# The sample attention's cache steps: three unrolled laps of 16 groups written as one register loop

## The chip, the cores and the metric

The kernel runs on one core of one Trainium2 chip. The metric is the device time of one execution in microseconds (us), the median of three runs. The core's engines each have their own instruction stream: TensorE (PE, with its weight loads shown as PEld), VectorE (DVE), ScalarE (ACT), GpSimd (POOL) and SyncE (SP), which here issues most of the DMAs. In rows of the profile a name with a "q" behind it (DVEq, SPq) is the sequencer of that engine, the part that reads the instruction stream, evaluates waits, does register arithmetic and branches.

## The reference

One inference step of a decoder layer. New tokens of a prompt (1024 and 16 meta tokens) and of 8 running sequences (8 tokens each) go through one projection. It feeds a pooling mixer and a latent attention of 8 heads. Then come an output projection and an MLP. The part that the change touches is the attention of the running sequences over their paged cache:

```python
def one_seq(args):                        # 8 sequences, 4096 cached positions each
    pt, qi, ci, kri = args
    c_all = concat([cache_kv_latent[pt].reshape(past, KV_LORA), ci])
    kr_all = concat([cache_k_rope[pt].reshape(past, QK_ROPE), kri])
    k = mla_keys(c_all, kr_all, w_uk, ...)      # project 256 -> 8 heads x 64, append rope, RMS norm
    s = einsum('qhd,khd->hqk', qi, k) * SCALE
    p = softmax(where(mask, s, -inf))
    ctx = einsum('hqk,kr->qhr', p, c_all)
    return einsum('qhr,rhv->qhv', ctx, w_uv)
```

## The kernel before

The program has four stages one after the other: the front (projections), the prompt attention, the sample attention and the tail (output projection and MLP). All five engines run each stage, and order among them is kept by counting semaphores alone: `eng.wait_ge(S[name], n)` holds an engine until the semaphore has reached n, and semaphores only ever grow, so n depends on the step.

**The sample attention.** The cache of a sequence is 32 pages of 128 positions. Four pages make a group, 8 groups make a sequence, and 64 groups (`NG`) make the stage. The groups go through a ring of 16 buffers (`RING`, two sequences). Step g is a software pipeline. In it PE turns group g's latents (eight transposes, L1294) and rope keys (L1304), and computes key norms and scores of group g-1 page by page. A page is 12 matmuls in three-pass form (helper `three_pass`, L104 to L106), six of 320 columns and six of 256. PE also does one rope product, and the context product of group g-12 (L1251, L1255) between page 1 and page 2. ACT copies the turned latents (`cTh`, L1358) and squares each page's keys (`sq`, L1340). DVE makes the low halves (`cTl`, L1416), adds rope to the scores (`summed`, L1404), reduces the squares (L1406) and closes a step with `krss` (L1491) and `var` (L1494). POOL scales scores and splits the context operand. Page j+2 on PE may start only when DVE has emptied the banks of page j (`S["summed"]`). SP loads a group's pages, four page numbers read from the page table (L1155), each followed by two DMAs (L1156, L1157), as soon as the context product has freed the buffer (`S["ctx"]`).

**How the steps are written out.** `steps` calls an engine's step function once for each g. The first 16 steps are the fill, in which `valid(x)` leaves out work of groups before the first. The last five drain the pipeline. The 48 between are all alike but for the wait counts, the page numbers and the sequence number, which are constants in the unrolled text. They are 16 steps (a lap) repeated three times.

**The tail** is written the other way already: its `steps` emits 6 steps as they are, and then a register loop `with eng.Fori(1, NS // LAP) as lap` (L1771) whose body is 6 steps, run seven times by PE, ACT and DVE. SP has a loop of its own there (L1743). Wait counts in such a body are worked out from the loop's register by the engine's sequencer (ALU_OP and FUSED_REGOPS in the rows), and the body ends with an addition and a COMPARE_BRANCH to its first instruction.

Of the kernel before, what the change touches and what calls it, by code (L numbers as in the profile page):

```python
# [48 lines left out]
NG = NSEQ * NPAGE // GP  # L49
GS = NPAGE // GP  # L50
RING = 2 * GS
# [1098 lines left out]
def load_pages(nc, A, C, c_tile, kr_tile, arrived, g):  # L1150


    cache, krope = A["cache_kv_latent"], A["cache_k_rope"]
    for j in range(GP):
        page = nc.sync.value_load(C["pages"][0:1, bass.ds(g * GP + j, 1)], min_val=0, max_val=cache.shape[0] - 1)  # L1155
        nc.sync.dma_start(c_tile[:, j, :], cache[bass.ds(page, 1), :, :].rearrange("a p n -> p (a n)")).then_inc(arrived, 16)  # L1156
        nc.sync.dma_start(kr_tile[:, j, :], krope[bass.ds(page, 1), :, :].rearrange("a p n -> p (a n)")).then_inc(arrived, 16)  # L1157


def sample_attention(nc, A, C, ps, B, arrived):  # L1160
# [7 lines left out]
    with ExitStack() as ctx:  # L1168
# [11 lines left out]
        S = {k: sem("sa_" + k) for k in (  # L1180
            "transposed", "hi", "lo", "krt", "krhi", "krlo", "q", "kn", "sq", "ssq", "rope", "ropec", "summed", "krsq", "krss",
            "var", "sd", "rinv", "scaled", "most", "newcopied", "pair", "lmax", "turned", "top", "spread", "gmax",
            "shifted", "exp", "prob_hi", "prob_lo", "const", "c_hi", "c_lo", "c_lo_end", "ctx", "ctx_copied", "folded", "rden", "ctxn",
            "mask0", "mask1", "mask", "zeros", "ones", "uk_hi", "uk_lo", "ukt", "ukt_c", "qr_hi", "qr_lo", "qt", "qt_hi", "qt_lo",
            "new", "s_new", "sums", "end")}
# [7 lines left out]
        @block.sync  # L1193
        def _(sp):
            def load(k, g):
                load_pages(nc, A, C, c_ring[k], kr_ring[:, k % GS], group_in[k], g)

            for k in range(EARLY, RING):
                if k >= GS:
                    sp.wait_ge(S["krt"], k - GS + 1)  # L1200
                    sp.wait_ge(S["krsq"], k - GS + 1)
                load(k, k)
            for g in range(RING, NG):
                sp.wait_ge(S["ctx"], g - RING + 1)
                load(g % RING, g)

        def steps(emit):

            def program(eng):
                for g in range(RING):  # L1210
                    emit(eng, g, g, 0, lambda x, g=g: 0 <= g - x, True)
                for g in range(RING, NG):
                    emit(eng, g % RING, g, g // RING, lambda x: True, True)
                for g in range(NG, NG + 5):
                    emit(eng, g % RING, g, g // RING, lambda x, g=g: g - x < NG, False)
            return program
# [927 lines left out]
```

## Time and profile before

| | |
|---|---|
| median of 3 runs | 2212.88 us (2212.47 to 2216.06) |
| the profiled execution | 2212.47 us, of which the span 2210.7 us |
| PE busy / DVE / ACT / POOL | 2093.6 / 1181.0 / 813.9 / 377.6 us |
| granted PE clock, mean over the span | 0.977 |
| sample attention, fill (16 steps) | 703.7 to 836.9 us |
| its three laps of 16 steps | 836.9 to 984.4, 1131.8 and 1279.3 us |
| its drain | to about 1321 us |
| tail | to the end |

The span is from the first to the last instruction, and the 1.8 us around it are outside the program's instructions. A lap's share of time is found by the starts of the first transposes (L1294) of steps 16, 32, 48 and of the first step after the last lap. Busy time of an engine is not its bound: what counts is which engine's idle time lies on the path to the end.

### The profile page before, as it was taken

To read this page: it belongs to the slowest core of one execution; us is meant where nothing else is said; L and a number is where in the kernel's file an instruction comes from. 1 tells how busy PE (TensorE), PEld (TensorE's weight loads), DVE (VectorE), ACT (ScalarE), POOL (GpSimd) and SP (SyncE) were. 2 spreads that over 40 slices of the span, in tenths; PEclk is the share of its full clock that TensorE was granted. 3 is DMA by queue.
4 is the path that set the end of the run, shared out by engine and by line. 5 is a ranking of instruction groups with operands and counts; after the bars stand their busy time and mean duration, and the time that the engine had idled before them with its cause. 6 is when DMAs were issued, how large, how long until landed. Compare 5 with 4: busy or idle time off the path is not lost. (4 is left out here: it accounts for less than half of the span.)

```text
span 2210.7 us, 35185 instructions
## 1 busy us (share of the span) xinstructions
PE 2093.6 (95%) x12673; PEld 1922.5 (87%) x12673; DVE 1181.0 (53%) x2358; ACT 813.9 (37%) x1585; POOL 377.6 (17%) x436
## 2 busy tenths in 40 slices
PE   6998999969988999999999979999999999999998
PEld 5887999958877999999999958898989998989997
DVE  3764311146765777677767744444454445454444
ACT  4552111145553556566656633322121112221111
POOL 1110000024441145355535501000000000000000
PEclk8999999989998999999999989999999999999999
DMA  4233222134422312222222107021111111111102
GB/s 151 85 85 83 59 79 80 64 102 130 122 73 61 89 32 63 71 63 65 64 71 63 39 32 259 1 77 39 58 38 57 38 38 38 57 38 57 38 19 86
DMA packets 146191, 152.69 MB, mean 69 GB/s; under 512 B 50695, under 2 KB 122103, under 8 KB 145022
## 3 DMA queue, kind: packets, MB, share of 16 engines
q1 hardware_dynamic: 140325, 128.28, 19.8%
q0 software_dynamic: 5728, 22.65, 3.3%
q8 instruction: 77, 1.26, 0.2%
q14 instruction: 61, 0.49, 0.1%
HBM read 124.77 MB, written 25.97 MB: 68 GB/s over the span
## 5 line engine op out<-in xcount | busy, mean ns | idle before, releaser
L104 PE MATMUL ps<-mh,f_w1h 128*128 128x384 f32 (+1 forms) x768 | 250.6, 326 | 0.0
L106 PE MATMUL ps<-mh,f_w1l 128*128 128x384 f32 (+1 forms) x768 | 250.5, 326 | 0.0
L105 PE MATMUL ps<-ml,f_w1h 128*128 128x384 f32 (+1 forms) x768 | 250.3, 326 | 0.0
L1340 ACT ACTIVATE sq<-ps 128x512 f32<-128x512 f32 x256 | 153.1, 598 | 231.1 <-PE ps L106 231.1
L1892 ACT ACTIVATE tail_room<-ps 128x384 f32<-128x384 f32 (+1 forms) x96 | 45.5, 474 | 502.1 <-PE ps L106 502.1
L1937 DVE TENSOR_TENSOR t_m<-t_m,ps 128x512 f32<-128x512 f32 x256 | 171.5, 685 | 107.0 <-PE ps L106 107.0
L105 PE MATMUL ps<-f_late_l,f_late_h 128*128 128x512 f32 x512 | 199.9, 390 | 0.0
L106 PE MATMUL ps<-f_late_h,f_late_l 128*128 128x512 f32 x512 | 199.8, 390 | 0.0
L104 PE MATMUL ps<-f_late_h 128*128 128x512 f32 x512 | 199.3, 389 | 0.0
L1917 DVE TENSOR_TENSOR tail_room<-tail_room 128x384 f32<-128x384 f32 (+1 forms) x96 | 51.5, 536 | 253.8 <-ACT tail_room L1892 253.8
L104 PE MATMUL ps<-wq,cTh 128*128 128x320 f32 x512 | 171.9, 336 | 2.1 <-DVE g_attn_b L1404 2.1
L1406 DVE TENSOR_REDUCE ss<-sq 128x8 f32<-128x512 f32 x256 | 172.8, 675 | 0.0
L105 PE MATMUL ps<-wq,cTh 128*128 128x320 f32 x512 | 159.3, 311 | 0.0
L106 PE MATMUL ps<-wq,cTl 128*128 128x320 f32 x512 | 158.7, 310 | 0.0
L104 PEld LDWEIGHTS ps<-mh,f_w1h 128*128 128x128 f32 x768 | 144.2, 188 | 1.9
L105 PEld LDWEIGHTS ps<-ml,f_w1h 128*128 128x128 f32 x768 | 144.2, 188 | 1.8
L106 PE MATMUL ps<-w_late,cTl 128*128 128x256 f32 x512 | 145.1, 283 | 0.0
L105 PE MATMUL ps<-w_late,cTh 128*128 128x256 f32 x512 | 144.8, 283 | 0.0
L1404 DVE TENSOR_TENSOR g_attn_b<-ps,g_attn_b 128x64 f32<-128x64 f32 x256 | 56.8, 222 | 164.1 <-ACT sq L1340 162.9
L106 PEld LDWEIGHTS ps<-mh,f_w1l 128*128 128x128 f32 x768 | 144.1, 188 | 0.0
L104 PE MATMUL ps<-w_late,cTh 128*128 128x256 f32 x512 | 143.5, 280 | 0.0
L106 PEld LDWEIGHTS ps<-f_late_h,f_late_l 128*128 128x128 f32 x512 | 96.1, 188 | 20.2
(348 smaller groups left out, 5051.7 us busy)
## 6 DMA issues: line engine op xcount, KB each, us to landing
f_raw<-in_w_ff SPq DMA_DIRECT2D x32, 1024.0 KB, 5.3
c_ring<-in_cache_kv_latent SPq DMA_DIRECT2D x192, 128.0 KB, 2.0
m_raw<-in_w_in SPq DMA_DIRECT2D x20, 512.0 KB, 4.0
gated<-gate POOLq DMA_DIRECT2D x8, 1088.0 KB, 5.2
pa_gm<-gated SPq DMA_DIRECT2D x16, 512.0 KB, 4.9
c_early<-in_cache_kv_latent SPq DMA_DIRECT2D x64, 128.0 KB, 2.0
fr_x<-in_x_prompt SPq DMA_DIRECT2D x8, 512.0 KB, 3.5
mixed<-pa_mixed SPq DMA_DIRECT2D x16, 256.0 KB, 2.1
```

What stands on the lines that cost most here:

```text
L104: nc.tensor.matmul(out, lh, rh, start=first, stop=False)
L105: nc.tensor.matmul(out, lh, rl, start=False, stop=False)
L106: return nc.tensor.matmul(out, ll, rh, start=False, stop=last)
L1340: nc.scalar.activation(sq[:, j % 2, :].rearrange("p (a n) -> p a n", a=2), ps[:, kn_bank(j):kn_bank(j) + 2, 0:HALF], ACT.Square).then_inc( ...
L1404: nc.vector.tensor_tensor(summed[:, p1, j * HQ:(j + 1) * HQ], ps[:, kn_bank(j), HALF:HALF + HQ], rope[:, p1, j * HQ:(j + 1) * HQ], ALU.add ...
L1406: nc.vector.tensor_reduce(ss[:, p1, j * H:(j + 1) * H], sq[:, j % 2, :].rearrange("p (h d) -> p h d", d=NOPE), AX.X, ALU.add).then_inc(S[" ...
L1892: nc.scalar.activation(z[:, a, 0:w], ps[:, 2 * par + a, 0:w], ACT.Relu).then_inc(S["relu"], 1)
L1917: nc.vector.tensor_tensor(z[:, a, 0:w], z[:, a, 0:w], z[:, a, 0:w], ALU.mult).then_inc(S["z"], 1)
L1937: nc.vector.tensor_tensor(part, part, ps[:, bank, :], ALU.add).then_inc(S["y"], 1)
```

## The change

The three laps become one loop body with a register counter, on SP, PE, ACT, DVE and POOL alike. Each engine has its own loop and its own register `lap`, 1 to 3. The body is the same 16 steps. The fill and the drain stay unrolled. No instruction that computes or moves data is added or taken away, and semaphores, buffers and the order of the work stay.

```diff
-            for g in range(RING, NG):
-                sp.wait_ge(S["ctx"], g - RING + 1)
-                load(g % RING, g)
+            with sp.Fori(1, NG // RING) as lap:
+                for k in range(RING):
+                    sp.wait_ge(S["ctx"], lap * RING + (k - RING + 1))
+                    load(k, lap * RING + k)
 
         def steps(emit):
 
             def program(eng):
                 for g in range(RING):
                     emit(eng, g, g, 0, lambda x, g=g: 0 <= g - x, True)
-                for g in range(RING, NG):
-                    emit(eng, g % RING, g, g // RING, lambda x: True, True)
+                with eng.Fori(1, NG // RING) as lap:
+                    for k in range(RING):
+                        emit(eng, k, lap * RING + k, lap, lambda x: True, True)
                 for g in range(NG, NG + 5):
                     emit(eng, g % RING, g, g // RING, lambda x, g=g: g - x < NG, False)
             return program
```

## Rows read from the trace of the kernel before

**Rows 1.** The page: engines over the span, PE and its clock in 40 slices.
```profile
PE 2093.6 (95%) x12673; PEld 1922.5 (87%) x12673; DVE 1181.0 (53%) x2358; ACT 813.9 (37%) x1585; POOL 377.6 (17%) x436
...
PE   6998999969988999999999979999999999999998
...
PEclk8999999989998999999999989999999999999999
```
**Rows 2.** Windows: the second ring lap, then one lap of the tail's loop.
```profile
core 0: us, PE busy (x) PEld busy (x) DVE busy (x) ACT busy (x) POOL busy (x), PEclk, DMA share, GB/s
...
984.40:1131.80 147.40, 144.34 (x1105) 140.83 (x1105) 104.53 (x265) 90.66 (x174) 69.14 (x74) 1.00 0.25 66
...
1687.50:1782.30 94.80, 94.80 (x497) 86.03 (x496) 45.45 (x69) 18.56 (x28) 0.00 (x0) 1.00 0.14 44
```
**Rows 3.** Waits in the first ring lap: PE, PEld and SP.
```profile
PE ps L1251 <- DVE prob_hl L1410: 3.1, 2, 1.5
...
PEld ps L1255 <- issue: 0.8, 2, 0.4
PEld ps L1304 <- issue: 0.8, 2, 0.4
...
SPq L1155 <- PE ps L1251: 39.4, 16, 4.7
```
**Rows 4.** Lines L1771 (tail loop) and L1936 (a wait in it): control instructions, ns.
```profile
L1771 DVEq FUSED_REGOPS  x7: 51/51/51, 1498.3 to 2067.7; - x7
...
L1771 ACTq COMPARE_BRANCH  x7: 40/45/45, 1587.0 to 2156.1; - x7
...
L1771 PEldq COMPARE_BRANCH  x7: 83/215/233, 1589.4 to 2158.5; - x7
...
L1771 DVEq COMPARE_BRANCH  x7: 50/56/72, 1593.1 to 2162.2; - x7
...
L1936 DVEq ALU_OP  x210: 40/40/40, 1508.4 to 2161.2; - x105
```
**Rows 5.** Timeline of DVE: an unrolled tail step, then the same one looped.
```profile
1491.86 1.24 DVE L1928 TENSOR_TENSOR f_late_l<-tail_room,f_late_h 128x384 fp32r<-128x384 f32 x2
1493.01 1.30 DVE L1937 TENSOR_TENSOR t_m<-t_m,ps 128x512 f32<-128x512 f32 x2
...
1586.80 1.23 DVE L1928 TENSOR_TENSOR f_late_l<-tail_room,f_late_h 128x384 fp32r<-128x384 f32 x2
1587.94 1.28 DVE L1937 TENSOR_TENSOR t_m<-t_m,ps 128x512 f32<-128x512 f32 x2
```
**Rows 6.** DMA queues: packets, MB, share; the second ring lap, then the whole span.
```profile
q8 instruction: 9, 0.15, 0.4%
q14 instruction: 11, 0.09, 0.2%
...
q8 instruction: 77, 1.26, 0.2%
```
**Rows 7.** DMA in 1600 to 2150 us, all queues; and landing of the ring's rope loads.
```profile
q1 hardware_dynamic: 14621, 23.78, 13.4%
issues: line engine op xcount, KB each, median us to landing
f_raw<-in_w_ff SPq DMA_DIRECT2D x22, 1024.0 KB, 5.3
...
DMA to landing us min/median/max: 1.6/1.8/4.3
```
**Rows 8.** Timeline of PE around its first branch, at 1589.4 us.
```profile
1589.41 0.39 PE L106 MATMUL ps<-f_late_h,f_late_l 128*128 128x512 f32 x1
...
1592.61 0.39 PE L1865 MATMUL ps<-f_late_h 128*128 128x512 f32 x1
```
**Rows 9.** Timelines across the end of the second ring lap: PE, then DVE.
```profile
1131.82 0.28 PE L106 MATMUL ps<-w_late,cTl 128*128 128x256 f32 x1
1131.94 1.04 PE L1294 MATMUL ps<-ident,c_early 128*128 128x128 f32 x8
...
1137.08 0.31 PE L104 MATMUL ps<-wq,cTh 128*128 128x320 f32 x1
...
1133.82 0.19 DVE L1494 TENSOR_TENSOR var<-ss,krss 128x32 f32<-128x32 f32 x1
1133.92 1.28 DVE L1416 TENSOR_TENSOR cTl<-ps,cTh 128x512 fp32r<-128x512 f32 x2
...
1135.32 0.21 DVE L1404 TENSOR_TENSOR g_attn_b<-ps,g_attn_b 128x64 f32<-128x64 f32 x1
```
**Rows 10.** Timeline of PE: two stalls; and the windows right behind and around them.
```profile
1285.80 0.52 PE L104 MATMUL ps<-wq,cTh 128*128 128x320 f32 x1 [2.07 <-DVE g_attn_b L1404]
...
880.13 0.39 PE L1251 MATMUL ps<-ch,prob_hl 128*128 128x258 f32 x1 [1.52 <-DVE prob_hl L1410]
...
1286.00:1289.40 3.40, 3.40 (x15) 3.40 (x15) 1.26 (x4) 0.43 (x1) 0.63 (x1) 0.50 0.00 0
...
876.00:882.00 6.00, 4.48 (x32) 3.76 (x31) 5.96 (x13) 4.42 (x8) 5.91 (x12) 1.00 0.12 28
```

## The prediction

> **What bounds the kernel now.** I read the page first. PE works 95% of the span at nearly the full clock, and nothing else comes near it [rows 1]. Next the windows of one ring lap: 16 steps take 147.4 us, PE is busy 144.3 of them, DVE 104.5, ACT 90.7, POOL 69.1 [rows 2]. Then the waits of a lap. PE stands 3.1 us for DVE's split of the probabilities, twice, and its weight loads wait 0.8 us at two places each for instructions to be issued [rows 3]. So this stage is a train of matmuls with small holes. Anything that delays another engine is free until a hole opens in that train, and what touches PE's own stream is paid at once.
>
> **What the change removes.** Program text, and with it nothing that PE waits for. PE's instructions come by DMA on the queue named instruction: 77 packets for the program, 1.26 MB, 16 KB each, and 9 of them in a ring lap [rows 6]. A lap has 1105 matmuls and as many weight loads, 2210 instructions, so a packet carries about 250. All this is fetched ahead: the issue waits of a lap are four of 0.4 us [rows 3], too few for nine packets, and the array does not stand for them, since its idle 147.4 - 144.3 = 3.1 us [rows 2] all have DVE as releaser [rows 3]. So I put the gain at zero.
>
> **What it adds: register arithmetic.** Every wait count now hangs on `lap`. The tail's loop shows the price: 40 ns for one ALU_OP on DVE, 51 ns for a fused one [rows 4]. Counting the waits in `dve_step` and `act_step` I get 15 to 20 a step, so some 0.6 to 0.8 us of a sequencer's time in a step of 147.4 / 16 = 9.2 us. Does it lie beside the engine's work? The tail has the same DVE code unrolled and looped [rows 5]. From the start of the pair L1928 to the start of the pair L1937 it is 1.15 us unrolled and 1.14 us looped, and the pair L1937 takes 1.30 and 1.28 us. The arithmetic is done while the engine works on the instruction before. PE gets 10 to 12 such counts a step. In the tail loop it is busy the whole 94.8 us of a lap all the same [rows 2]. In the ring the pairs are shorter (320 and 256 columns against 384 and 512), and eight transposes still start 0.11 us apart ((1.04 - 0.27) / 7, taking 0.27 us for one, [rows 9]), so the sequencer can hand out a pair in 0.11 us where a page needs 0.12 to 0.15. I take zero. The bounds are zero and 1 us a lap, for waits that do end last.
>
> SP: its arithmetic grows by two or three operations a page, at most 4 x 3 x 0.05 = 0.6 us a group. It waits 39.4 us in 16 groups now [rows 3], 2.5 us each, so that is covered. If the cover were gone, a late load would show as a wait of PE on a DMA. Its branch is covered by the same slack.
>
> **What it adds: two taken branches on each engine.** The body runs three times, so the branch is taken twice, after step 31 and after step 47. The branch itself is 45 to 233 ns [rows 4]. What matters is whether the target is still there. The tail's PE body has 497 matmuls, 993 instructions with their weight loads, so four or five packets. In 550 us of that loop there is no instruction packet on any queue [rows 7]. So a body of about 1000 is kept. The ring's body on PE is 2210 and the arithmetic, nine to ten packets, and no row of this trace shows whether that much is kept. DVE's body is at least 265 and its separate waits and arithmetic, I estimate 500 to 600, against 69 instructions and as much arithmetic in the tail's. The Trainium skill ("Runtime: NRT & Kernel Launch", Instruction fetch mechanics) speaks against this change here: it puts PE's instruction memory at 2048 instructions and the others' at 512, and says that a taken branch whose target has left it must fetch the page before going on. By that page PE, DVE and SP miss at both branches, and a body that fitted would cost only the branch; that the tail's body of 993 stays is in accord with it, and no run shows the limit.
>
> What would a miss cost? A demand fetch is at least a small load and one long packet. The nearest rows are the ring's 16 KB rope loads, 1.6 to 4.3 us to landing with a median of 1.8 [rows 7], and an instruction packet on the queue of PE, 0.4% of 16 x 147.4 us over 9 packets, which is 1.05 us [rows 6]. For PE that makes 2.9 at the low end (median load and packet) and 5.4 at the high end (longest load and packet). I take 4.0, just under the middle, as a request from a sequencer that stands still has nothing queued ahead of it. For DVE a packet is 8 KB (0.09 MB in 11), 0.2% of the same over 11, or 0.43 us. That gives 2.2 to 4.7, and I take 3.4.
>
> PE at the branch: its sequencer runs ahead of the array. The first branch of the tail is executed at 1589.4 [rows 4] and the last matmul of that lap starts at 1592.61, 14 matmuls later [rows 8]. In the ring 14 matmuls of page 3 are worth about 1.9 us (12 of them span 1.6). So the hole in PE's train is 4.0 + 0.2 - 1.9 = 2.3 us. With the bounds it is 1.2 to 3.7, and nothing if the body is kept.
>
> DVE at the branch: `var` starts at 1133.82 and the next step's `cTl` at 1133.92 [rows 9]. I add 0.1 us for the addition and the branch, and 0.3 for the first instruction behind it: in the tail DVE's seven branches are (2162.2 - 1593.1) / 6 = 94.85 us apart, so the sixth was at 2067.35, and the fused operation that begins the body comes at 2067.7 [rows 4]. Then `cTl` starts at 1133.82 + 0.4 + 3.4 = 1137.6, 3.7 us late. `summed` of page 0 follows it and ends at 1135.53 now. PE's page 2 needs it at 1137.08 [rows 9], slack 1.5 us. A hole of 3.7 - 1.5 = 2.2 us would open there, if PE were in time. PE is 2.3 us late itself by then, so it is the same hole and not a second one. ACT is earlier in its chain and misses, if it does, in the shadow of the same.
>
> Sum: 2 x 2.3 = 4.6 us, everything else zero. The profiled execution took 2212.47 us with a span of 2210.7. It would be 2217.1. The median stands 0.4 above it, which makes **2217.5 us**.
>
> **Rivals.**
> *The bodies are kept, or their heads are fetched in time.* Then each branch costs PE nothing, as in the tail: 2212.9 to 2214 us with some arithmetic on waits that end last. For it: the tail's loop without one hole in PE. Against it: 2210 instructions are more than twice what was shown to be kept.
> *The hole halves the clock.* After an idle 2.07 us the granted clock was 0.50 for the next 3.4 us, so 1.2 instead of 2.4 GHz; after an idle 1.52 us it stayed at 1.00 [rows 10]. A hole of 2.3 us is above the first. Each such fall costs 1.7 us (3.4 us at half speed), and the sum is 4.6 + 2 x 1.7 = 8.0 us: 2220.9. Against it: at the lap's end PE has been busy without a pause, and the 2.07 us came soon after another stretch with holes.
> *The arithmetic is paid in every step.* If PE's sequencer falls behind by ten operations of 0.03 us a step, 48 steps cost 15 us: 2228. It decides if a page's pair of 0.12 us leaves no room. The transposes at 0.11 us and the tail at full PE speak against it.
> *Faster.* The one place where the loop could gain is the fetching: if the four issue waits of 0.4 us a lap came from instruction packets, cost the train their full length, and another place of the packet boundaries moved them away, that is 1.6 us a lap and 4.8 in all, 2208.1. It decides only if all of it is real. Against it: PE's idle time in a lap is the 3.1 us with DVE as releaser and nothing else.
>
> **How the numbers follow.** A measurement of this kernel can tell about 0.2% from no change, 4.4 us. Chances: a hole at both branches with the clock kept 0.45 (1.2 to 3.7 us each, 2.4 to 7.4 us together, of which a little under half lies within 4.4 us), bodies kept or hidden 0.24, holes with a halved clock 0.20, arithmetic in every step 0.06, faster 0.05. The likeliest is the first, 2217.5. Slower by over 0.2% is 0.24 of the first, the 0.20 and the 0.06, so 0.50. Within 0.2% are 0.21 of the first and the 0.24, so 0.45. Faster is the last case, 0.05. The range reaches down to 2212.0, which takes in nearly all of the bodies-kept case, and up to 2223.5, the halved clock with longer holes. What stays outside is the every-step case, the gains, and the longest holes.
>
> **What would show it.** In the changed profile: a hole in PE's timeline at steps 32 and 48 of about 2.3 us in front of or soon after the first transposes, released by issue and not by another engine, and nothing like it at step 16. DVE's `cTl` there should be late by 3 to 4 us. The laps should read 147.4 us and one hole each. Instruction packets on PE's queue should still be nine or ten a lap. If the body is kept, they are missing in the second and third lap, and the laps are 147.5 us. The tail's laps should stay at 94.8 us. I would be wrong if holes show at other steps, if PE waits on `summed` all along a lap, or if SP's loads become what the transposes wait for.

## The result, and the profile after

The loop takes 2226.18 us (median, 2225.45 to 2230.14, five runs); the kernel before took 2214.03 us beside it (2212.47 to 2216.06, five runs). The ratio is 1.0059, with a 95% interval of 1.0046 to 1.0074. The profiled execution took 2224.16 us. The forecast was 2217.5 with a range up to 2223.5, so the median lies 8.7 us above the first and 2.7 above the second.

The page of the kernel after, lines that answer to [rows 1, 6]:

```profile
span 2222.2 us, 36454 instructions
...
PE 2101.2 (95%) x12673; PEld 1929.6 (87%) x12673; DVE 1172.5 (53%) x2358; ACT 813.6 (37%) x1585; POOL 379.8 (17%) x436
...
PEclk9998999989998999999999998999999999999999
...
q8 instruction: 82, 1.34, 0.3%
q14 instruction: 76, 0.62, 0.1%
```

The matmuls are the same 12673, and PE is busy 7.6 us longer, which means that some of them ran at a lower clock. The program did not get shorter to fetch: 82 packets against 77 on PE's queue. A ring lap has 10 or 11 of them, as forecast.

Windows of the first and the second ring lap and of one tail lap, against [rows 2]:

```profile
837.90:990.50 152.60, 147.57 (x1106) 143.87 (x1104) 102.23 (x267) 91.46 (x176) 69.96 (x74) 0.98 0.24 65
990.50:1140.30 149.80, 144.75 (x1104) 140.96 (x1104) 101.62 (x266) 90.57 (x174) 69.94 (x74) 1.00 0.25 65
1694.00:1788.80 94.80, 94.80 (x498) 86.00 (x497) 45.46 (x69) 18.55 (x28) 0.00 (x0) 1.00 0.14 44
```

The tail's lap is as it was. The ring's laps take 152.6 and 149.8 us where the second lap of before took 147.4, and the first has a mean clock of 0.98. To find the places I took the time from the first transposes (L1296, start of their first weight load) of one step to those of the next, for all 64 steps, and subtracted that of before. From step 16 to step 62 it is 433.6 us against 425.1. The whole difference stands in ten steps; the others agree to 0.02 us. The fourth column is a second profiled execution of the same kernel.

| step | before | after | after, again | what it is |
|---|---|---|---|---|
| 20 | 11.17 | +1.83 | +0.31 | context stall |
| 28 | 11.19 | +1.74 | +1.73 | context stall |
| 31 | 8.66 | +1.68 | +1.86 | branch |
| 32 | 8.67 | +0.09 | +0.11 | DVE behind its branch |
| 36 | 11.17 | +0.31 | +1.83 | context stall |
| 44 | 11.19 | +0.23 | +1.74 | context stall |
| 47 | 8.66 | +1.73 | +1.88 | branch |
| 48 | 8.67 | +0.38 | -0.04 | DVE behind its branch |
| 52 | 11.17 | +0.33 | +0.32 | context stall |
| 60 | 11.19 | +0.22 | +0.21 | context stall |
| sum | | +8.5 | +10.0 | |

Waits over the three laps, first of the kernel after, then of the kernel before (us in total, times, longest):

```profile
PE ps L1253 <- DVE prob_hl L1412: 10.8, 6, 1.9
DVE cTl L1418 <- issue: 6.4, 2, 3.4
...
PE ps L1296 <- issue: 2.9, 2, 1.5
```
```profile
PE ps L1251 <- DVE prob_hl L1410: 9.2, 6, 1.5
```

Two kinds of thing are new. The two waits "issue" at the transposes are the branches. The stall before the context product ("context stall" from here on) was there before, once in 8 steps, and each is now 0.2 to 0.3 us longer.

**The branches.** Control instructions at the line of the loop (ns: shortest/median/longest), the first ones of POOL and ACT behind their first branch, then PE's and DVE's timelines behind it, against [rows 4, 9]:

```profile
L1213 PEldq COMPARE_BRANCH  x3: 83/3506/3550, 986.7 to 1286.6; - x3
L1213 ACTq COMPARE_BRANCH  x3: 40/45/45, 989.3 to 1289.2; - x3
L1213 DVEq COMPARE_BRANCH  x3: 55/63/72, 990.9 to 1290.8; - x3
...
L1213 POOLq FUSED_REGOPS  x1: 68/68/68, 986.6 to 986.6; - x1
...
L1213 ACTq FUSED_REGOPS  x1: 56/56/56, 991.7 to 991.7; - x1
```
```profile
988.80 0.28 PE L106 MATMUL ps<-w_late,cTl 128*128 128x256 f32 x1
990.51 1.09 PE L1296 MATMUL ps<-ident,c_early 128*128 128x128 f32 x8 [1.43 <-issue]
```
```profile
990.79 0.19 DVE L1496 TENSOR_TENSOR var<-ss,krss 128x32 f32<-128x32 f32 x1
...
994.03 1.29 DVE L1418 TENSOR_TENSOR cTl<-ps,cTh 128x512 fp32r<-128x512 f32 x2 [3.05 <-issue]
```

PE's sequencer stands 3.5 us in each taken branch; the one that is not taken, at the loop's end, takes 83 ns. The array sees the matmul of 988.80 followed by one of 990.51. DVE's branch takes 63 ns and its next instruction comes 3.05 us late, 3.4 at the second branch. ACT's branch is at 989.3 and the first instruction of its body at 991.7, 2.4 us behind it; with the hint of e4 below it is 0.2 us. That miss lies in the shadow of PE's, as the prediction said it would. SP's is 2.5 and 2.7 us, covered by its slack. POOL's branch is at 986.3, and it goes on after 0.3 us. Counted in the trace between two branches, a body has 2342 instructions on PE, 657 on SP, 455 on DVE, 388 on ACT and 147 on POOL; the tail's have 1051, 124 and 73 on PE, DVE and ACT. The first four bodies of the ring are fetched again; POOL's and those of the tail go on within 0.3 us. That is in line with the Trainium skill ("Runtime: NRT & Kernel Launch", Instruction fetch mechanics), cited in the prediction, with its 2048 for PE. Its 512 for the other engines is no usable length here, since 455 and 388 were missed. The same section speaks of a window of two pages of 256 instructions, and a body of either size can lie across three; where the pages of this program begin, no trace here shows.

**The clock.** Windows behind three context stalls:

```profile
882.20:885.60 3.40, 3.40 (x16) 3.40 (x16) 1.01 (x2) 0.00 (x0) 3.06 (x2) 0.50 0.20 51
...
957.30:960.70 3.40, 3.40 (x16) 3.40 (x15) 1.16 (x2) 0.00 (x0) 3.21 (x2) 0.50 0.06 17
...
1034.20:1037.60 3.40, 3.40 (x27) 3.40 (x27) 1.58 (x5) 0.60 (x1) 3.06 (x3) 1.00 0.11 28
```

At 882.2 and 957.3 the granted clock is 0.50 (1.2 GHz) for 3.4 us and PE gets through 16 matmuls where it does 27 at 1.00 (2.4 GHz). Those are the steps with +1.83 and +1.74 instead of +0.31 and +0.22, so a fall costs 1.52 us. It is the same phenomenon as in [rows 10], at stalls and not at the branches: behind the branch holes the clock stayed at 1.00. So the laps divide as follows: branches with what DVE adds 3.9 us, longer stalls 3 x 0.31 + 3 x 0.22 = 1.6 us, clock falls 2 x 1.52 = 3.0 us, together 8.5. In the second execution it is 3.8 + 1.6 + 3 x 1.52 = 10.0.

**Why the stall is longer.** The chain in front of it is POOL's: it scales scores (L1525) when DVE's `rinv` is ready, then runs four shifts, the low half of the context operand, and the casts of the probabilities that DVE splits for PE. DVE's `rinv`, then POOL's control instructions and timeline, of the kernel after, then of before:

```profile
1021.95 0.34 DVE L1455 RECIPROCAL rinv<-sd 128x32 f32<-128x32 f32 x1
...
L1520 POOLq FUSED_REGOPS  x1: 46/46/46, 1022.3 to 1022.3; - x1
L1523 POOLq ALU_OP  x1: 32/32/32, 1022.4 to 1022.4; - x1
...
1022.55 0.63 POOL L1525 TENSOR_TENSOR prob<-g_attn_b,rinv 128x256 f32<-128x256 f32 x1 [2.32 <-DVE rinv L1455]
1023.14 5.18 POOL L1541 TENSOR_TENSOR prob<-prob,gmax 128x512 f32<-128x512 f32 x4
```
```profile
1015.66 0.34 DVE L1453 RECIPROCAL rinv<-sd 128x32 f32<-128x32 f32 x1
...
1016.08 0.63 POOL L1523 TENSOR_TENSOR prob<-g_attn_b,rinv 128x256 f32<-128x256 f32 x1 [2.06 <-DVE rinv L1453]
```

From the end of `rinv` to the scaling it was 0.08 us and is 0.25 (0.23 to 0.25 in all six trains). `pool_step` waits for `rinv` first and for `summed` and `ctx` behind it. In the loop the counts of these two are worked out from `lap`, and the trace has that arithmetic (L1520, L1523) behind the wait for `rinv`, the wait that ends last. Here it is not hidden: 0.17 us for each train of POOL's. The stalls grew by 0.32 and 0.23 us, so that is a little over half. The traces place the rest. `rinv` itself ends 4.45 us into the step where it was 4.37, which is 0.08 more, in every run with the loop on all engines and in none with it on PE, POOL or DVE alone (ACT and SP were not tried alone). And from the end of DVE's split to PE's matmul it is 0.13 us in place of 0.06 at the first stall of a sequence, which e1, with PE's loop alone, shows too.

### The profile page after: what moved, and what is told of

It reads as the page before. It is cut to its first block and busy times, and to the rows that moved or that the text cites. A ratio compares the mean times of both kernels' runs of the same rounds, so it can differ in the third digit from the quotient of the medians.

```text
span 2222.2 us, 36454 instructions
## 1 busy us (share of the span) xinstructions
PE 2101.2 (95%) x12673; PEld 1929.6 (87%) x12673; DVE 1172.5 (53%) x2358; ACT 813.6 (37%) x1585; POOL 379.8 (17%) x436
```

## The experiments

Ratios are to the kernel before on the same chip, with 95% intervals. "Stall" is the time between the starts of the matmuls on either side of a context stall, 1.80 us before, 2.12 and 2.04 after (first and second of a sequence).

**Which engine's loop costs what.** The loop is written for one engine alone:

```diff
+                if emit in (pe_step,):       # or (pool_step,), or (dve_step,)
+                    with eng.Fori(1, NG // RING) as lap:
+                        for k in range(RING):
+                            emit(eng, k, lap * RING + k, lap, lambda x: True, True)
+                else:
+                    for g in range(RING, NG):
+                        emit(eng, g % RING, g, g // RING, lambda x: True, True)
```

> Loop on PE alone; ACT, DVE, POOL and SP keep their unrolled text. Theory (two causes): PE's taken branch waits for its target's instructions, 3.5 us less what the array still has queued, so a hole of 1.7 us in front of the transposes of steps 32 and 48 and 1.7 to 1.8 us per branch in the step times; the stalls at the context product of steps 20, 28, 36, 44, 52, 60 keep their 1.80 us, as POOL's text is the old one, and no clock fall follows them. Time +3.5 us against before. Rival A (the stalls grow by PE's own arithmetic): they read 2.0 to 2.1 us here too, and the time is +5 us or, with clock falls, +8 us. Rival B (what hurts is DVE's late text at the branch): no hole above 0.5 us at 32 and 48.

Measured: 2219.08 us, 1.0019 (1.0010 to 1.0028). Waits of PE over the laps:

```profile
PE ps L1256 <- DVE prob_hl L1415: 9.4, 6, 1.6
...
PE ps L1299 <- issue: 3.4, 2, 1.8
```

Steps 31 and 47 are +1.87 and +2.04, no other more than 0.08, and the clock does not fall. The branch hole belongs to PE's loop alone, and PE's own register arithmetic costs 0.2 us in three laps.

> Loop on POOL alone. Theory: POOL's arithmetic sits between a wait and the score scaling (L1523 before), which then starts 0.25 us late once in each sequence, and all six stalls at the context product grow from 1.80 to 2.04 to 2.13 us; no hole at steps 32 and 48. The steps themselves cost 6 x 0.25 = 1.5 us, and stalls of that length are now and then followed by 3.4 us at half clock (1.5 to 1.7 us each, none to six of them), so +1.5 to +9 us, about +5. Rival A (PE's or DVE's arithmetic makes the stalls longer): stalls stay at 1.80 and the time is that of before. Rival C (text that has moved, not arithmetic): the time moves with no step of the ring longer.

Measured: 2216.99 us, 1.0008 (0.9999 to 1.0017). The stalls are 1.97 and 1.95 us:

```profile
PE ps L1256 <- DVE prob_hl L1415: 10.1, 6, 1.7
```

There is no hole at a branch and no fall of the clock. POOL's loop lengthens the stalls by 0.16 and 0.14 us, the time from `rinv` to the scaling being 0.25 us here too: about half of what the full loop does, less than expected. Behind stalls of this length the clock did not fall.

> Loop on DVE alone. In the changed kernel DVE's first instruction behind the branch came 3.0 to 3.4 us late. Theory: with PE in time this opens a hole of its own, since DVE's slack to page 2 of steps 32 and 48 is only 1.5 us: step 32 and 48 longer by 1 to 1.8 us each, and DVE's arithmetic makes the stalls at the context product 0.03 to 0.12 us longer (1.83 to 1.92), with no clock fall behind them. Time +2.5 to +4 us. Rival (DVE's late text is hidden): steps 32 and 48 within 0.4 us of before, time +0.5 us.

Measured: 2217.69 us, 1.0013 (1.0004 to 1.0022). DVE's timeline and PE's waits:

```profile
989.44 1.29 DVE L1421 TENSOR_TENSOR cTl<-ps,cTh 128x512 fp32r<-128x512 f32 x2 [2.89 <-issue]
```
```profile
PE ps L1256 <- DVE prob_hl L1415: 9.1, 6, 1.5
...
PE ps L104 <- DVE g_attn_b L1409: 2.9, 2, 1.6
```

DVE's miss alone opens a hole at page 2, +1.61 in step 32 and +1.91 in step 48, and leaves the stalls alone. In the full loop only 0.1 to 0.4 us of it shows, because PE is late already.

**Is it the text or the branch?** Three loops of one trip each, so that no branch is taken:

```diff
+                for turn_ in range(1, NG // RING):
+                    with eng.Fori(turn_, turn_ + 1) as lap:
+                        for k in range(RING):
+                            emit(eng, k, lap * RING + k, lap, lambda x: True, True)
```

> Three loops of one trip in place of one loop of three, on all engines: the same register arithmetic, the text as long as unrolled, no branch taken. Theory: stalls at the context product 2.04 to 2.13 us as in the changed kernel, no hole at steps 32 and 48; +1.5 us and clock falls, so +1.5 to +9, the changed kernel less 3.5 to 4 us. Rival D (the branch and its fetch are all of the loss): the time of before within 1 us.

Measured: 2214.97 us, 1.0001 (0.9992 to 1.0010), every step of the laps as before. The trace shows why the expectation does not apply: with one trip the register is a constant and the counts were worked out when the program was built, so no arithmetic is left (a lap of DVE has 333 instructions, against 455 in the loop). What it tests is smaller than planned: an untaken branch and moved text cost nothing.

**Take the miss away.** The loops get a hint ahead of the branch that its target will be needed:

```diff
-                with eng.Fori(1, NG // RING) as lap:
+                with nc.Fori(1, NG // RING, engines=OrderedEngineSet([eng.engine]), hint_back_edge=True) as lap:
```

> The changed kernel with a prefetch hint for the branch at the head of every iteration on each engine, so that the target is fetched before it is needed. Theory: PE's branch takes about 0.2 us in place of 3.5 and DVE's cTl is not late; the holes at 32 and 48 go; stalls at the context product stay at 2.04 to 2.13. The changed kernel less 3.5 to 4 us. Rival D: the time of before. Rival E (the target cannot be kept next to the running text): branch still over 3 us, time of the changed kernel.

Measured: 2227.77 us, 1.0065 (1.0051 to 1.0079), no better than the loop as it was. Control instructions at the loop, the waits, and the window behind one stall:

```profile
L1214 PEldq COMPARE_BRANCH  x3: 88/358/397, 986.5 to 1287.1; - x3
```
```profile
PE ps L1254 <- DVE prob_hl L1413: 10.8, 6, 1.9
...
PE ps L1952 <- PEq L1169: 4.5, 1, 4.5
```
```profile
1032.30:1035.70 3.40, 3.40 (x16) 3.40 (x17) 1.44 (x4) 0.00 (x0) 3.17 (x2) 0.50 0.03 5
```

The miss is gone: the branch takes 0.36 and 0.40 us, and steps 31, 32, 47 and 48 are as before (+0.00). The saved 3.9 us went elsewhere. The clock fell behind five of the six stalls, three more than in the first execution of the kernel after (4.6 us), and where the stage changes to the tail PE waits 4.5 us; there the kernel after has

```profile
PE ps L1951 <- PEq L1168: 1.8, 1, 1.8
```

That is 2.7 us more, and the half clock behind it lasts 20.5 us instead of 17.1. All engines meet at that line (L1169, L1168 in the kernel after), and the control instructions there tell who comes last. DVE's last operation before it, then its control instruction at the line, in e4 and in the kernel after:

```profile
1329.04 0.48 DVE L1643 TENSOR_SCALAR room<-ps,rden 64x256 f32<-64x256 f32 x1
L1169 DVEq DRAIN  x2: 10/72/135, 1332.1 to 1332.5; - x2
```
```profile
1328.07 0.48 DVE L1642 TENSOR_SCALAR room<-ps,rden 64x256 f32<-64x256 f32 x1
L1168 DVEq DRAIN  x2: 19/259/499, 1328.1 to 1328.9; - x2
```

PE's own is at 1326.0 in e4, so PE is long there, although the row names its sequencer. It is DVE's sequencer that comes 2.6 us behind the end of its last operation, where in the kernel after it is there beforehand; e9, with the same hint, shows the same. The delay is near DVE's 3.05 us behind its branch, but it stands at no branch. Why the hint brings it about was not tried.

**Shorten the stall.** The waits of POOL are put in the order in which they end, so that all arithmetic comes ahead of the last:

```diff
-                pool.wait_ge(S["rinv"], g - 1)
-                pool.wait_ge(S["summed"], 4 * g - 4)
                 if valid(2 + RING):
                     pool.wait_ge(S["ctx"], g - (RING + 1 - max(0, 2 - k)))
+                pool.wait_ge(S["summed"], 4 * g - 4)
+                pool.wait_ge(S["rinv"], g - 1)
```

> The changed kernel with the three waits in front of POOL's scaling of the scores in the other order, the one that ends last (rinv) at the end, so that the arithmetic for the other two is done before it ends. Theory: the stalls at the context product fall from 2.13 / 2.04 to about 1.95 / 1.90 us, and at that length no clock fall follows them (with POOL's loop alone they were 1.97 / 1.95 and none did), while the holes at steps 32 and 48 stay. Time: before + 3.9 + 0.8, so +4.7 us, 4 to 8 less than the changed kernel. Rival (the falls come from the loop's whole pattern, not from the length of the stall): time of the changed kernel, falls as before.

Measured: 2222.08 us (2214.62 to 2224.50), 1.0027 (1.0016 to 1.0037). The stalls are 2.00 and 1.94 us, and the clock fell behind none of them:

```profile
PE ps L1253 <- DVE prob_hl L1412: 10.2, 6, 1.7
```

The laps are 4.7 us above before instead of 8.5 to 10.0: branches 3.7, stalls 1.0. The branch holes stay (+1.78 and +1.70). What is left of the longer stall is what was said of `rinv` (0.08 us later) and of PE (0.07 at every other stall); from `rinv` to the scaling it is 0.14 us, still 0.06 more than before.

> The changed kernel with both the prefetch hint and POOL's wait order (rinv last). Against the hint alone the stalls at the context product should fall from 2.13 / 2.04 to 2.00 / 1.94 us, 0.8 us in all, and nothing else changes. Theory (falls of the clock follow stalls of over about 2.0 us, 1.5 us each): no fall in laps 1 to 3, no hole at steps 32 and 48; time before + 1.0 from the steps, so +0.5 to +3 us, 8 to 11 us less than the hint alone. Rival (the falls are a matter of the loop, not of the stall's length): 0.8 us less than the hint alone, +11 us.

The order of e6 and the hint of e4 together. Measured: 2220.25 us (2217.82 to 2224.16), 1.0029 (1.0019 to 1.0040).

```profile
PE ps L1254 <- DVE prob_hl L1413: 10.2, 6, 1.7
```
```profile
1028.00:1031.40 3.40, 3.40 (x28) 3.40 (x27) 3.40 (x5) 0.60 (x1) 2.79 (x2) 1.00 0.16 42
```

The laps are only 1.0 us above before: no branch hole, no fall, stalls 2.02 to 1.95. Of the other 4.3 us of the profiled execution 2.7 are the change of stage, where PE waits 4.5 us as in e4. Against e4 the one edit of the wait order takes five falls away, 5 x 1.52 = 7.6 us, and with the shorter stalls the laps are 8.2 us less. The medians stand 12.7 (e4) and 5.9 us (e9) above the kernel before on the same chip, 6.8 apart.

**Move the stall in the unrolled kernel.** Three edits of the kernel before were meant to lengthen or shorten the stall with no loop at all. The first puts two tiny operations in front of POOL's scaling once a sequence:

```diff
+                if loading and last_of(k, 4, valid):
+                    for i in range(2):
+                        nc.gpsimd.tensor_tensor(turn[:, i:i + 1], eps[0:1, :], eps[0:1, :], ALU.mult)
```

> The unrolled kernel before, with no loop at all, and two one-element operations put on POOL in front of the scaling that the probabilities wait for, once in a sequence (the unused scratch turn is written; nothing else changes). Theory: POOL's chain is 0.26 to 0.31 us later, the six stalls grow from 1.80 to 2.06 to 2.11 us, and 3.4 us at half clock follow several of them, 1.5 us each. Time +1.7 us and 1.5 for each fall, so +3 to +10 us with no loop in it. Rival (the length of the stall is not what sets off the fall): +1.7 us and no falls.

Measured: 2246.75 us, 1.0139 (1.0125 to 1.0154), far more than expected of either. The same DVE instruction in the timelines of e7, of before, and of the kernel after:

```profile
1035.43 5.78 DVE L1478 TENSOR_TENSOR most<-most,prob 128x256 f32<-128x256 f32 x1
```
```profile
1021.08 1.05 DVE L1478 TENSOR_TENSOR most<-most,prob 128x256 f32<-128x256 f32 x1
```
```profile
1027.30 1.31 DVE L1480 TENSOR_TENSOR most<-most,prob 128x256 f32<-128x256 f32 x1
```

Elsewhere this instruction takes 0.41 us. Next to POOL's train it lasts longer, in before and in the loop until 0.29 us behind the end of POOL's four shifts, which makes 1.05 and 1.31 us. In e7 the shifts end 0.31 us later against it than in before, and only 0.05 later than in the loop; there it was held through the shifts, the low half and most of the casts, and each sequence paid 4.7 to 6.0 us. PE then waits on page 2 too (holes of 2.2 to 2.9 us, start to start), and the clock falls in all six sequences. So this run says nothing of the context stall's length alone, but it shows how near the edge the place is. The Trainium skill ("GPSIMD Engine Reference", 1. Specifications) says that GpSimd shares its SBUF interfaces with VectorE and that DVE instructions with two SBUF inputs contend; this instruction has two, and the 5.78 against 0.41 us agree.

The second lets DVE make the first split ahead of its work on page 0 (`split_prob(0)` before `scores_and_norms(0)`):

```diff
+            if split:
+                split_prob(0)
             scores_and_norms(0)
```

> The unrolled kernel before, with DVE's first split of the probabilities put ahead of the score addition and the norm reduction of page 0 in its step, once in a sequence; the same instructions. DVE's split starts 0.73 us earlier (5.00 in place of 5.73 us into the step). Theory: what lengthened the stall in the changed kernel shortens it here: the six stalls at the context product read about 1.1 us in place of 1.80, and the time is 5 us less than before (0.2%), the fill's stall of 3.7 us shorter too. Rival (PE then waits for what was put back, the score addition of page 0): the hole moves behind the context product to page 2, no gain.

Measured: 2215.68 us, 0.9999 (0.9990 to 1.0008), the stalls 1.81 us as before.

```profile
1027.28 1.60 DVE L1399 TENSOR_TENSOR prob_hl<-prob,prob_hl 128x512 fp32r<-128x512 f32 x1
```

The split starts earlier and takes 1.60 us instead of 0.88, and ends where it did; the 5 us expected did not come. It is not DVE's order that sets the stall.

The third moves POOL's low half of the context operand behind the casts:

```diff
-            if valid(LAG - 1) and loading:
+                if valid(LAG):
+                    low_context(LAG)             # behind the casts of the next step
...
+            if valid(LAG - 1) and loading and not last_of(k, 4, valid):
+                low_context(LAG - 1)
```

> The unrolled kernel before with POOL's split of the context operand moved behind its four probability casts, in the one step of a sequence where it stood before them; same instructions. Theory (POOL's chain up to the last cast sets the end of the stall, since DVE's split gets through only then): the casts start up to 2 us earlier and the stall at the context product falls from 1.80 to 1.0 to 1.3 us, then set by the split of the context operand; 7 x 0.6 = 4 us, so -2 to -5 us (ratio 0.998). Rival (the context operand becomes the late one): stalls of 1.8 us or more, released by cl, no gain or slower.

Measured: 2246.17 us, 1.0144 (1.0129 to 1.0160).

```profile
1035.84 3.94 DVE L1494 TENSOR_TENSOR var<-ss,krss 128x32 f32<-128x32 f32 x1
```
```profile
PE ps L1251 <- DVE prob_hl L1410: 24.6, 6, 4.1
```

An instruction of 0.19 us, again with two SBUF inputs, takes 3.94 us while POOL runs its casts and the low half without a pause. The casts did start earlier, but the stall grows by 2.6 us to 4.4, and the clock falls in all six sequences. The theory failed. The rival had the loss right and its cause wrong: the wait is still for DVE's split and not for the low half.

**How firm is one profile?** The two kernels again, unchanged, on one chip.

> The changed kernel, a second look. Theory: steps 31 and 47 again 1.7 us longer, stalls again 2.13 / 2.04, as these follow from the program; clock falls behind a number of the six stalls that may differ from the two of the first look, as the window of the clock does not start with the program. A time of 2226 +/- 3 us with two to five falls. Rival: exactly the same two falls.

> The kernel before, a second look. Theory: six stalls of 1.80 us, no clock fall behind any of them, ring laps of 147.5 us again; what differs from the first look is the start, the fill's step 12 and the start of the tail, by 1 to 4 us. Rival: a clock fall behind some of the 1.80 us stalls too, which would take the falls out of the account of the change.

Measured: 2225.63 and 2211.74 us, spans 2223.6 and 2210.0. Before repeats itself to 0.1 us over the laps, with no fall of the clock. After has the same branch holes and the same stalls, but three falls instead of two and at other steps (table above). Waits of PE, first after, then before:

```profile
PE ps L1253 <- DVE prob_hl L1412: 10.8, 6, 1.8
...
PE ps L1296 <- issue: 3.2, 2, 1.6
```
```profile
PE ps L1251 <- DVE prob_hl L1410: 9.1, 6, 1.5
```

**Stall length and the clock.** All profiled executions but e7 and e10, in which DVE was held for microseconds; each has six context stalls in the laps.

| stall, start to start | kernels | falls of the clock |
|---|---|---|
| 1.78 to 1.82 us | before, again, e3, e5, e8 | 0 of 30 |
| 1.81 to 1.88 | e1 | 0 of 6 |
| 1.94 to 2.02 | e2, e6, e9 | 0 of 18 |
| 2.03 to 2.13 | after, again, e4 | 10 of 18 |
| other holes, at a branch or at page 2: 1.61 to 2.06 | after, again, e1, e5, e6 | 0 of 10 |

The last line keeps the table from being read as a limit: a hole of 2.06 us at e1's second branch left the clock at 1.00, and of the stalls of 2.03 us and more eight did too.

## Why the prediction was wrong, step by step

- **The bound and the gain of zero: right.** PE's train sets the laps, and a shorter text saved nothing: PE's instruction packets went from 77 to 82, since the body is fetched at every trip.
- **The base.** The sum starts from a median of 2212.88. Beside the changed kernel the one before took 2214.03, so 1.15 of the 8.7 us between forecast and median are not the change. For the change itself the forecast was 4.6 us and the measurement 12.15.
- **Two taken branches: the mechanism was right, the size a little high.** The fetch with the branch was put at 4.2 us and took 3.51 and 3.55; the sequencer's lead was put at 1.9 us and was 2.2 (branch at 986.7, last matmul of the lap in the array until about 988.9). The hole was 2.3 in the sum, and steps 31 and 47 grew by 1.68 and 1.73 us. DVE came 3.05 and 3.4 us late where 3.7 was forecast, and it is the same hole but for 0.1 to 0.4 us; e5 shows what it costs without PE's. Sum 3.9 us, forecast 4.6. The counts of arithmetic were put about twice too high for DVE and ACT (15 to 20 a step, the trace has 125 and 119 in 16 steps), so DVE's body is 455 and not 500 to 600; that did no harm, it missed all the same.
- **The step that failed: the register arithmetic.** In the prediction's words, "I take zero", with bounds of 0 and 1 us a lap "for waits that do end last". The lengths were counted on PE, DVE, ACT and SP. POOL's waits were not gone through, and POOL has a place where arithmetic stands behind the wait that ends last, on the chain to PE's only stall. It makes a little over half of the longer stall, `rinv` and PE itself the rest. The direct cost, 1.6 us in three laps, is inside the bound. What it triggers is not: stalls of 2.03 us and more, behind which the clock fell two or three times in six, 3.0 to 4.6 us more. With the wait order changed (e6) the falls and 0.6 of the 1.6 us are gone, with no other edit.
- **The rival "the hole halves the clock": the right phenomenon at the wrong place.** It looked for it at the branch holes, where it did not occur (1.71 to 2.06 us, start to start, none fell). That its time of 2220.9 is nearer to the measured one is luck. A fall was put at 1.7 us and costs 1.52. [rows 10] held both numbers, an idle time of 1.52 us kept and one of 2.07 fallen (the first is 1.80 from start to start), and the first is the context stall itself. To ask what happens if that stall grows by 0.3 us was the missing question.
- **Nothing in every step, SP covered, tail unchanged: right.** Steps outside the ten agree to 0.02 us, and the tail's laps read 94.8 us.
- **Open.** The laps account for 8.5 to 10.0 of the 12.15 us between the medians. Outside them both profiled executions of after are 3.0 us longer than before's first, in the fill (+0.9, -0.1), the drain (0.0, +1.8) and the tail (+2.1, +1.3), with the half clock at the tail's start lasting 17.1 instead of 13.7 us. But e3 and e8, which take no branch in the ring, show as much in their profiled executions (+3.5 and +4.5 us), at medians equal to before's. So a part of it is how single executions differ, before's two being at the low end of its runs; e6's twelve runs even part into four of 2214.6 to 2218.8 us and eight of 2221.6 to 2224.5. Whether the loop adds anything there is not settled. Also argued and not shown: that it is the length of the stall, and not what PE does around it, that decides on the clock. The edit that should have shown it in the unrolled kernel (e7) moved too much else. The context stalls of the table, e6 against after and e4 against e9 speak for length; that eight of 18 stalls of 2.03 to 2.13 us and a branch hole of 2.06 left the clock alone says that length is not all of it.

No version with a loop beat the kernel before. Of those with the loop on all engines e9 comes nearest in the laps (+1.0 us) and loses 2.7 us at the change of stage.

## What to carry to other kernels

Before unrolled steps become a register loop, count each engine's body with its arithmetic, and charge a taken branch whose body was not kept with the fetch less the sequencer's lead (here 3.5 less about 2 us on PE). Then go through every engine's waits, also those of one that is 17% busy, and ask for each which ends last and what is computed behind it; emit that wait last. Where a stall of the bounding engine is already near the length at which its clock has been seen to fall, a few tenths added to it cost several times their own length, so price the stall, not only the hole that you are adding.

## What the runs showed of the hardware

- Behind context stalls of up to 2.02 us, start to start, the clock never fell (0 of 54), behind those of 2.03 to 2.13 us it did 10 times in 18, each time 3.4 us at 0.50, or 1.52 us lost. It is no limit of the chip that this shows: a branch hole of 2.06 us had no fall.
- A DVE instruction that reads two operands from SBUF can be held through several POOL operations in a row: 0.41 us alone, 1.05, 1.31 and 5.78 us beside them, and 3.94 for one of 0.19. In e7 a shift of a few tenths of a microsecond cost 5 us in each sequence.
- Bodies of 2342 instructions on PE, 657 on SP, 455 on DVE and 388 on ACT were waited for at a taken branch (3.5, 2.5, 3.0 and 2.4 us); bodies of 1051 on PE, 147 on POOL, 124 on DVE and 73 on ACT were not.
- The hint at the branch removed the miss (3.5 to 0.4 us on PE), and DVE's sequencer came 2.6 us late at the next change of stage.
